# Products of decays and inputs taken two units at a time, in a fused state space and attention block

## The reference, cut to what matters

```python
def step(state, inp):
    xc, ac, bc, cc = inp
    acum = jnp.cumsum(ac, axis=1)
    seg = jnp.where(causal, acum[:, :, None] - acum[:, None, :], -jnp.inf)
    scores = jnp.einsum('btgn,bsgn->btsg', cc, bc)[..., None] * jnp.exp(seg)
    y_diag = jnp.einsum('btsgh,bsghp->btghp', scores, xc)
    y_off = jnp.einsum('btgn,bghpn->btghp', cc, state) * jnp.exp(acum)[..., None]
    w_end = jnp.exp(acum[:, -1:] - acum)
    new_state = (state * jnp.exp(acum[:, -1])[..., None, None]
                 + jnp.einsum('bsgn,bsghp->bghpn', bc, xc * w_end[..., None]))
    return new_state, y_diag + y_off
```

## Time and profile before

| | |
|---|---|
| time, three runs | 1519.07, 1519.62, 1519.64 us, median 1519.62 |
| time of the profiled execution | 1519.86 us |
| span of the profiled execution | 1518.0 us |
| PE, PEld, DVE busy | 1504.9, 1204.2, 971.3 us |
| ACT, POOL busy | 672.2, 99.4 us |
| scan on TensorE | from 85.9 us to 334.5 us of the span |

### The profile page before, as it was taken

The page is one execution under the profiler, slowest core; times in us unless marked ns, Lnnn a source line. Parts: engine busy times, 40 slices in busy tenths (PEclk is TensorE's granted clock), DMA queues, the critical chain, the costliest instruction groups (busy, mean ns, idle before and its releaser), DMA issues.

```text
span 1518.0 us, 18644 instructions
## 1 busy us (share of the span) xinstructions
PE 1504.9 (99%) x7454; PEld 1204.2 (79%) x7454; DVE 971.3 (64%) x1254; ACT 672.2 (44%) x964; POOL 99.4 (7%) x66
## 2 busy tenths in 40 slices
PE   9999999999999999999999999999999999999998
PEld 5888787778788877778888876688888888888887
DVE  5869899997895888854488267735544443432435
ACT  4656567754543677654212445523432323222232
POOL 0000001011300000032000000000210000000110
PEclk9999999999999999999999999999999999999999
DMA  9344354434684322222212342122323222222223
GB/s 392 116 153 153 117 177 137 139 111 167 225 297 170 116 88 88 70 74 96 84 64 77 108 143 84 56 83 84 111 83 110 85 107 88 104 97 91 97 98 125
DMA packets 49310, 184.68 MB, mean 122 GB/s; under 512 B 3988, under 2 KB 21012, under 8 KB 33096
## 3 DMA queue, kind: packets, MB, share of 16 engines
q1 hardware_dynamic: 32400, 174.91, 32.1%
q10 hardware_dynamic: 16824, 8.58, 2.4%
HBM read 174.98 MB, written 4.30 MB: 118 GB/s over the span
## 4 chain that ended last, share of the span: by engine, by line
PE 92%; DVE 4%; ACT 2%; issue 1%; DMA 1%; POOL 0%; ACTq 0%; DVEq 0%
PE bank L737 25%; PE bank L739 25%; PE bank L738 24%; PE zz L1117 1%; PE bank L1071 1%; PE tt L1048 1%; PE tt L886 1%; DVE wlo L1355 1%; PE bank L991 1%; PE bank L993 1%; PE bank L992 1%; PE zz L1205 1%; PE zz L1059 1%; PE bank L1218 1%; PE tt L858 1%
## 5 line engine op out<-in xcount | busy, mean ns | idle before, releaser
L737 PE MATMUL bank<-HH,whi 128*128 128x512 f32 x1344 | 543.4, 404 | 0.6 <-ACT whi L2234 0.6
L739 PE MATMUL bank<-HH,wlo 128*128 128x512 f32 x1344 | 525.0, 391 | 0.0
L738 PE MATMUL bank<-HL,whi 128*128 128x512 f32 x1344 | 524.1, 390 | 0.0
L1355 DVE TENSOR_TENSOR wlo<-raw,whi 128x2048 fp32r<-128x2048 f32 (+2 forms) x127 | 262.6, 2068 | 92.6 <-ACT whi L2151 83.4
L737 PEld LDWEIGHTS bank<-HH,whi 128*128 128x128 f32 x1344 | 252.6, 188 | 61.1 <-issue 12.0
L739 PEld LDWEIGHTS bank<-HH,wlo 128*128 128x128 f32 x1344 | 252.2, 188 | 54.4
L738 PEld LDWEIGHTS bank<-HL,whi 128*128 128x128 f32 x1344 | 252.9, 188 | 49.0 <-issue 2.6
L2151 ACT ACTIVATE whi<-raw 128x2048 fp32r<-128x2048 f32 (+1 forms) x107 | 202.4, 1891 | 143.1 <-PE bank L739 116.5
L2814 POOL TENSOR_TENSOR SRT<-SRT 128x512 f32<-128x512 f32 x47 | 84.0, 1787 | 907.8 <-ACT SRT L2185 906.1
L739 PE MATMUL bank<-FH,wlo 128*128 128x512 f32 x176 | 68.5, 389 | 0.0
L738 PE MATMUL bank<-FL,whi 128*128 128x512 f32 x176 | 68.5, 389 | 0.0
(11 more groups left out here) (352 smaller groups left out, 2153.4 us busy)
## 6 DMA issues: line engine op xcount, KB each, us to landing
raw<-wstream SPq DMA_DIRECT2D x113, 1024.0 KB, 4.9
aslot<-tstream SPq DMA_DIRECT2D x24, 512.0 KB, 3.5
AD<-tstream SPq DMA_DIRECT2D x24, 512.0 KB, 5.2
A<-astream SPq DMA_DIRECT2D x8, 1024.0 KB, 17.7
AC<-scratch ACTq DMA_DIRECT2D x16, 512.0 KB, 5.4
QD<-QD SPq DMA_DIRECT2D x16, 256.0 KB, 3.8
raw<-wstream SPq DMA_DIRECT2D x4, 768.0 KB, 4.2
X<-xT SPq DMA_DIRECT2D x2, 1024.0 KB, 6.6
```

The costliest lines, as they stand in the source:

```text
L737: e.matmul(o, wh[:, k, c], hi[:, kb0 + k, :], start=first and k == 0, stop=False)
L738: e.matmul(o, wh[:, k, c], lo[:, kb0 + k, :], start=False, stop=False)
L739: x = e.matmul(o, wl[:, k, c], hi[:, kb0 + k, :], start=False, stop=last and k == kb - 1)
L1355: x = e.tensor_tensor(wlo[:, i % 2, c], raw[:, i % 2, c], whi[:, i % 2, c].bitcast(F32), ALU.subtract)
```

## The change

Products of decays and inputs are issued for two units in one place: spells now stand in steps 1, 3, 5, 7, 9, 10, 11, 13 and 15 (units 0+1, 2+3, 4+5, 6+7, 8+9, 10, 11, 12+13, 14+15). Odd units and unit 10 go to `aux[2]`, the other even ones to `aux[3]`, the bank of C times state. E and XD get a third buffer in the region of `Y[:, 12:16]` (units below 10) and one in `XS[0]` (unit 14), and YT a second buffer at the same places. VectorE reads units at the steps in `Y_READ`. Line 858 has a new wait on `s_dsk` (`to_free`), the spell waits on `s_tyo` before it writes `aux[3]`, and ScalarE and VectorE wait on `s_yd` before they write a slot of E or XD again (`slot_free`). No operation is added or removed.

```diff
--- before.py
+++ after.py
@@ -342,6 +342,24 @@
     one = lambda name, k: cv[:, VOFF[name][0] + k:VOFF[name][0] + k + 1]
     eps_ap, eps2_ap = eps[:, 0:1], eps[:, 1:2]
     flat = lambda t: t.rearrange("p a b -> p (a b)")
+
+
+    spare = lambda t, k: t[:, k:k + 4, :]
+    e_of = lambda t: t[:, 0:2, :].rearrange("p a (b n) -> p (a b) n", n=128)
+    xd_of = lambda t: t[:, 2, :].rearrange("p (h n) -> p h n", h=8)
+    yt_of = lambda t: t[:, 3, :].rearrange("p (q n) -> p q n", q=4)
+    slot_of = lambda u: u % 3 if u < 10 else {14: 3}.get(u, (u + 1) % 2 if u < 15 else 1)
+    early, late = spare(Y, 12), spare(XS[0], 0)
+    Es, XDs = [E[0][:, :, :], E[1][:, :, :], e_of(early), e_of(late)], [XD[0][:, :, :], XD[1][:, :, :], xd_of(early), xd_of(late)]
+    e_at, xd_at = lambda u: Es[slot_of(u)], lambda u: XDs[slot_of(u)]
+    yt_at = lambda u: YT[:, :, :] if u % 2 == 0 or u == 11 else yt_of(early if u < 10 else late)
+    slot_free = lambda u: max([v + 1 for v in range(u) if slot_of(v) == slot_of(u)] + [0])
+
+    Y_SPELL = {u: (u,) if u in (10, 11) else (u - 1, u) for u in [1, 3, 5, 7, 9, 10, 11, 13, 15]}
+    y_bank = lambda u: aux[2] if u % 2 or u == 10 else aux[3]
+    Y_READ = {2: (0,), 3: (1,), 4: (2, 3), 6: (4,), 7: (5,), 8: (6, 7), 10: (8, 9), 11: (10,), 12: (11,), 14: (12,), 15: (13,), 16: (14, 15)}
+    to_free = lambda u: max([v + 1 for n in Y_SPELL if n < u for v in Y_SPELL[n] if y_bank(v) is aux[3]] + [0])
+    y_free = lambda u: max([v + 1 for v in range(u) if y_bank(v) is aux[2]] + [0])
     ones0 = HL[:, 7, 0:128].bitcast(F32)
     dts = flat(XD[0][0:32, :, :])
     xb, dd, ac = flat(YT[0:32, :, :]), flat(EA[0:32, :, :]), flat(E[0][0:32, 0:4, :])
@@ -854,6 +872,8 @@
                 if 0 <= u < 16 and c > 0:
                     w.wait_ge(s_st, 3 * g + c)
                     w.wait_ge(s_tyo, 3 * g + c - 1)
+                    if to_free(u):
+                        w.wait_ge(s_dsk, to_free(u))
                     for q in range(4):
                         x = e.matmul(aux[3][:, 128 * q:128 * q + 128], flat(ST[:, 2 * q:2 * q + 2, :]),
                                      Cc[g % 2][:, 128 * c:128 * c + 128], start=True, stop=True)
@@ -877,13 +897,16 @@
                     w.wait_ge(s_cb, min(g + 1, 4))
                     sum_of(f"y{g - 1}", aux[1], n=3)
                 yield
-                if 0 <= u < 16:
-                    w.wait_ge(s_m, u + 1)
-                    w.wait_ge(s_xd, u + 1)
-                    w.wait_ge(s_dsk, u)
+                for v in Y_SPELL.get(u, ()):
+                    w.wait_ge(s_m, v + 1)
+                    w.wait_ge(s_xd, v + 1)
+                    if y_bank(v) is aux[3]:
+                        w.wait_ge(s_tyo, 3 * g + c)
+                    elif y_free(v):
+                        w.wait_ge(s_dsk, y_free(v))
                     for h in range(8):
                         q, o = h // 2, 64 * (h % 2)
-                        x = e.matmul(aux[2][o:o + 64, 128 * q:128 * q + 128], XD[u % 2][:, h, :], E[u % 2][:, h, :],
+                        x = e.matmul(y_bank(v)[o:o + 64, 128 * q:128 * q + 128], xd_at(v)[:, h, :], e_at(v)[:, h, :],
                                      start=True, stop=True)
                     x.then_inc(s_yd, 1)
                 if u < 15 and cv_ == 0:
@@ -1486,16 +1509,16 @@
             for u in range(-1, 19):
                 g, c = divmod(u, 4)
                 gv, cv_ = divmod(u + 1, 4)
-                if 0 < u < 17:
-                    p, q0 = u - 1, (u - 1) // 4
+                for p in Y_READ.get(u, ()):
+                    q0 = p // 4
                     xs, cs = XS[q0 % 2], slice(128 * (p % 4), 128 * (p % 4) + 128)
-                    y = quads(aux[2])
-                    w.wait_ge(s_yd, u)
+                    y = quads(y_bank(p))
+                    w.wait_ge(s_yd, p + 1)
                     if p % 4:
                         w.wait_ge(s_tyo, 3 * q0 + p % 4)
-                        e.tensor_tensor(YT[:, :, :], y, YT[:, :, :], ALU.add).then_inc(s_dsk, 1)
-                        w.wait_ge(s_dsk, u)
-                        y = YT
+                        e.tensor_tensor(yt_at(p), y, yt_at(p), ALU.add).then_inc(s_dsk, 1)
+                        w.wait_ge(s_dsk, p + 1)
+                        y = yt_at(p)
                     o = VOFF["m_d"][0] + 4 * q0
                     for q in range(4):
                         x = e.scalar_tensor_tensor(xs[:, q, cs], xs[:, q, cs], cv[:, o + q:o + q + 1], y[:, q, :],
@@ -1511,14 +1534,16 @@
                                         ALU.mult).then_inc(s_cb, 1)
                     w.wait_ge(s_cb, g + 1)
                     w.wait_ge(s_ee, u + 1)
-                    e.tensor_tensor(E[u % 2][:, :, :], E[u % 2][:, :, :], CB[:, c, :].unsqueeze(1).to_broadcast([128, 8, 128]),
+                    e.tensor_tensor(e_at(u), e_at(u), CB[:, c, :].unsqueeze(1).to_broadcast([128, 8, 128]),
                                     ALU.mult).then_inc(s_m, 1)
                 yield
                 if 0 <= u < 16:
                     if c > 0:
                         w.wait_ge(s_to, 3 * g + c)
                         w.wait_ge(s_ea, 3 * g + c)
-                        e.tensor_tensor(YT[:, :, :], quads(aux[3]), EA[:, :, :], ALU.mult).then_inc(s_tyo, 1)
+                        if u == 13:
+                            w.wait_ge(s_y, 12)
+                        e.tensor_tensor(yt_at(u), quads(aux[3]), EA[:, :, :], ALU.mult).then_inc(s_tyo, 1)
                     if c == 0:
                         w.wait_ge(s_ts, 3 * g + 1)
                         w.wait_ge(s_to, 3 * g)
@@ -1530,8 +1555,10 @@
                         e.tensor_tensor(ST[:, :, :], ST[:, :, :], heads(aux[4][:, :]), ALU.add).then_inc(s_st, 1)
                 yield
                 if u < 15:
-                    hs, xd = slice(8 * gv, 8 * gv + 8), XD[(u + 1) % 2]
+                    hs, xd = slice(8 * gv, 8 * gv + 8), xd_at(u + 1)
                     w.wait_ge(s_tx, u + 2)
+                    if slot_free(u + 1):
+                        w.wait_ge(s_yd, slot_free(u + 1))
                     e.tensor_tensor(xd[:, :, :], heads(aux[0]), dtk[:, cv_, hs].unsqueeze(2).to_broadcast([128, 8, 64]),
                                     ALU.mult).then_inc(s_xd, 1)
                     if cv_ < 3:
@@ -2325,12 +2352,15 @@
                 if u < 15:
                     w.wait_ge(l_ac, 16 * (u + 2))
                     w.wait_ge(s_tk, 1)
-                    w.wait_ge(s_yd, u)
+                    if slot_free(u + 1):
+                        w.wait_ge(s_yd, slot_free(u + 1))
+                    if u == 13:
+                        w.wait_ge(s_y, 12)
                     for h in range(8):
-                        x = e.activation(E[(u + 1) % 2][:, h, :], AC[:, h, :], ACT.Relu, scale=-1.0,
+                        x = e.activation(e_at(u + 1)[:, h, :], AC[:, h, :], ACT.Relu, scale=-1.0,
                                          bias=atk[:, cv_, 8 * gv + h:8 * gv + h + 1])
                     own(x)
-                    e.activation(E[(u + 1) % 2][:, :, :], E[(u + 1) % 2][:, :, :], ACT.Exp, scale=-1.0).then_inc(s_ee, 1)
+                    e.activation(e_at(u + 1), e_at(u + 1), ACT.Exp, scale=-1.0).then_inc(s_ee, 1)
                 if g > 0 and c == 1:
                     w.wait_ge(s_sqa, SA_AT[f"y{g - 1}"] + 1)
                     w.wait_ge(s_y, 4 * g - 1)
```

## The result

The changed kernel takes 1541.80 us (median of four runs, 1540.21 to 1542.22) against 1519.54 us for the kernel before, measured beside it (1519.07 to 1519.64). The ratio is 1.0146, interval 1.0134 to 1.0158: 22.3 us slower. The profiled execution took 1542.22 us, the longest of the four, with a span of 1540.4 us. The lines have moved: 858 is now 878, 886 is 909, 853 is 871, 1496 is 1519, 1501 is 1524, 1514 is 1537, 1521 is 1546.

The account below looks back on a forecast made before the run. TensorE, busy 99% of the span, was taken as the bound, so its waits are paid in full. Waits 16.5, joins -1.5, steps 12 to 15 0 and clock 4.4 gave +19.4 us: 1539.0 us, range 1531 to 1545.

Parts of the forecast that it names:

- rival (b): All gaps drop the clock, or waits are longer since VectorE also loses time: 1541 to 1546 us, chance 0.15.
- What the joining removes: Seven joined spells on TensorE save 0.3 us each (bounds 0 and 0.4): five 1.5 us, all seven 2.1 us.
- The new wait of line 858: TensorE idles for VectorE's read in steps 2, 6 and 10: 3.9, 6.3 and 6.3 us, sum 16.5 us.
- Steps 12 to 15: TensorE already waits for VectorE here; small gains and losses taken as 0, bounds -0.7 and +1 us.
- The clock: TensorE's clock falls to half after the two 6.3 us waits, 2.2 us each: 4.4 us, bounds 0 and 9.
- Costed at nothing: Waits on s_yd for slots, on s_tyo before even units (some tenths at most), and late reads of 14 and 15.
- Sum: Whole kernel: 16.5 - 1.5 + 0 + 4.4 = +19.4 us, giving 1539.0 us; chance 0.55.
- Rival (a): The waits come but the clock stays: +15.0 us, 1534.6 us, chance 0.22.
- (c): VectorE isn't late at steps 2, 6 and 10; only joins are left, -2.1 to -2.8 us, about 1517.2; chance 0.05.
- (d): Joins give nothing: 1541 us with the waits, 1519.6 with (c); chance 0.02 for the two together.

Follow-up runs that it names:

- experiment 3: Changed kernel with units 0, 4, 8 and 12 in aux[1] in place of aux[3], all seven joins kept: 1516.98 us, ratio 0.9985.
- experiment 6: Changed kernel with only the joins of units 2+3, 6+7 and 14+15: 1518.15 us, ratio 0.9993.
- experiment 7: As version 3, but units 12 and 13 have their spells apart: 1517.01 us, ratio 0.9984.
- Experiment 1: Kernel before, with only a wait added at line 858 of steps 2, 6 and 10 for VectorE's read: 1542.63 us, ratio 1.0156.
- experiment 5: Changed kernel, banks kept, with VectorE's reads of units 0, 4, 8 and 12 moved to stage 4 of the step before: 1520.34 us, ratio 1.0006.
- version 3: The kernel of experiment 3: changed kernel with units 0, 4, 8 and 12 in aux[1]: 1516.98 us, ratio 0.9985.
- experiment 2: Changed kernel with 16, 27 and 27 unread dense passes before the waits of steps 2, 6 and 10: 1535.93 us, ratio 1.0110.
- experiment 4: As version 3, but unit 0 stays in aux[3], leaving only the wait of step 2: 1522.55 us, ratio 1.0024.

## Why the prediction came true, point by point

The measured 1541.8 us lie in the range, but inside the band of rival (b) (1541 to 1546) and 2.8 us over the forecast (1539.0). The range took in both, so the time alone doesn't tell them apart; the traces do, and what happened to the clock is what (b) says.

- **What the joining removes.** Right, and shown by experiment 3: 0.37 us for each of the five joins in steps 0 to 9 (0.29 and 0.34 in the traces of experiments 6 and 7), where I had taken 0.3 from a pair pace of 0.117 us (a pair is two passes side by side) and given 0.4 as the bound. The pace of a pair is 0.11: the second unit adds 1.97 - 1.09 = 0.88 us, not 0.94.
- **The new wait of line 858.** Right in mechanism, place and size: 3.97, 6.45 and 6.51 us against 3.9, 6.3 and 6.3, 16.9 against 16.5. Experiment 1 shows that it makes the loss alone, and experiments 3 and 5 that either another bank or another place for the read takes it away. The anchors were right as well: VectorE paused for ScalarE 1.12 us before the read of step 2, so the read that left step 1 brought nothing there.
- **Steps 12 to 15.** Taken as 0, measured +0.6 (22.4 less 21.8 over the traces' ends). One term was mis-sized: I had line 1546 ready before the spell of 12+13, but the spell waited 0.95 us for it, since line 1537 before it took 2.32 us there and not 1.28. Line 878 of step 14 then stood 22.55 us after line 871 of step 12, where it was 21.55 us before: 1.0 us later, and the last join takes 0.4 of it back. The rows of VectorE and GpSimd at this place, of the kernel before, the changed kernel and version 3:

```profile
311.03 1.28 DVE L1514 TENSOR_TENSOR E<-E,CB 128x1024 f32<-128x1024 f32 x1
307.94 3.29 POOL L2814 TENSOR_TENSOR SRT<-SRT 128x512 f32<-128x512 f32 x1 [46.15 <-ACT SRT L2185]
...
331.82 2.32 DVE L1537 TENSOR_TENSOR E<-E,CB 128x1024 f32<-128x1024 f32 x1
329.76 3.30 POOL L2844 TENSOR_TENSOR SRT<-SRT 128x512 f32<-128x512 f32 x1 [56.15 <-ACT SRT L2212]
...
308.13 1.22 DVE L1541 TENSOR_TENSOR E<-E,CB 128x1024 f32<-128x1024 f32 x1
306.08 4.43 POOL L2848 TENSOR_TENSOR SRT<-SRT 128x512 f32<-128x512 f32 x1 [46.79 <-ACT SRT L2216]
```

A GpSimd addition runs at this place in every trace. Where the read still stands before the multiplication (before, experiments 1 and 6) the multiplication takes 1.28 or 1.29 us. Where it has left, the two instructions overlap, and one of them takes 1.1 us longer: VectorE's in the changed kernel and experiments 2, 4, 5 and 7, GpSimd's in version 3. That they hold each other up fits all nine traces, but no run takes the addition away. The prediction moved the multiplication 1.04 us earlier and kept its length.

- **The clock.** That the clock falls and is paid for was right, and is shown by experiment 2. The count was wrong: three falls, not two, at 6.6 us instead of 4.4. I had read the 4.6 us at the end of the trace as a level that must be passed, although one row can only say that this long was enough once. In step 10 of the changed kernel the clock fell at 276.5 us (windows above), 2.0 us after the end of TensorE's last pass (273.46 + 1.02). The rule that I had set beside it, from the Trainium skill ("TensorE: Matmul & The Clock Gate", "Why this matters for your kernels", on idle gaps between bursts), pointed to the third fall and to 1541 us. The trace agrees with it: the clock was at half after each of the three waits. The price of one fall, taken from the first six passes as 2.2 us, is also the mean of 1.7, 1.95 and 2.95. That is luck in part: it came from the start of the kernel, and single falls cost from 1.5 us (experiment 4) to 2.95 us.
- **Costed at nothing.** The waits on `s_yd` for the slots and the late reads of units 14 and 15 show in no wait of TensorE. The wait on `s_tyo` shows once, the 0.9 us above.
- **Sum.** Forecast +19.4 us, measured +22.3 us. Of the 2.9 between them 2.2 are clock (three falls instead of two), 0.6 are steps 12 to 15, 0.4 the waits, less 0.4 for the joins; 0.1 is left over. Rival (b), all gaps drop the clock, is what happened. Rival (a) falls by the windows of the changed kernel, (c) by the waits in its timeline, (d) by experiment 3.

## What to carry to other kernels

Before a buffer is given to two users, look at *when* its reader stands at the read in its own order, not at how busy the reader is on average: VectorE was busy 64% of the span, and still 3 to 6 us behind TensorE at the place that counted, which nothing had asked for until then. A wait of 3.5 us or more of a saturated TensorE cost more than its length here, as the clock went with it. And the gain of grouping small products is small (0.3 to 0.4 us for each joined spell), so one wait of a few microseconds takes more than all of it; with a bank that nobody asks for before the read is done the same grouping does pay, 2.1 us.

## What the runs showed of the hardware

- The half clock lasted unevenly long once TensorE worked again, and so a fall had no fixed price. In the changed kernel it was 3.4, 3.9 and 5.9 us after waits of 3.97, 6.45 and 6.51 us (each twice the loss worked out above), in experiment 1 5.5, 3.2 and 4.5 us, in experiment 4 3.1 us. The wait of step 2 alone cost 1.5, 1.7 and 2.7 us of clock in the three traces.
- When the clock fell was as uneven. In these seven cases it fell 2.0 to 4.6 us after the end of TensorE's last pass (2.0 in step 10 of the changed kernel, 2.1 in step 2 of experiment 1, 3.5 in experiment 4). In step 2 of the changed kernel it fell only when work had gone on again for about 0.7 us: the mean clock over 129 to 131 us is 0.68.
- In three traces (changed kernel, experiments 1 and 4) 3.5 to 3.8 us of idle TensorE were followed by a half clock. In steps 12 to 15, idle times of up to 1.4 us were not. Between 1.4 and 3.5 us no wait was measured.
- Seventy dense passes whose result nobody reads (16, 27 and 27), put into the three waits, made the kernel 5.9 us faster than waiting idle.
- A VectorE multiplication of 128x1024 and a GpSimd addition of 128x512 that overlapped took 2.32 and 3.30 us in five traces and 1.22 and 4.43 us in one. Where they met only at the end (before, experiments 1 and 6) they took 1.28 or 1.29 and 3.3 us.
